# Modulation steps of three parts moved from VectorE to GpSimd, in a two-block transformer kernel

## The reference

```python
c_act = jax.nn.silu(c)
for i in range(DEPTH):                      # 2 layers
    mod = c_act @ ada_w[i] + ada_b[i]       # (1, 1024) @ (1024, 6144)
    shift_t, scale_t, gate_t, shift_c, scale_c, gate_c = split(mod, 6)
    h = rmsnorm(x, norm_g[i, 0]) * (1.0 + scale_t) + shift_t
    y = gla_mixer(h, ...) if i == 0 else diff_mixer(h, ...)
    x = x + gate_t * y
    h = rmsnorm(x, norm_g[i, 1]) * (1.0 + scale_c) + shift_c
    x = x + gate_c * (square(relu(h @ mlp_w1[i])) @ mlp_w2[i])
```

## Time and profile before

| | |
|---|---|
| median of 3 runs | 1410.97 us |
| the profiled execution's own time | 1412.19 us |
| its span, first to last instruction | 1410.4 us |
| mean granted TensorE clock | 0.989 |
| PE, DVE, ACT, POOL busy | 96%, 68%, 47%, 6% |
| chain that ended last | PE 83%, DVE 8%, ACT 3% |

### The profile page before, as it was taken

How to read it: one execution, slowest core, us unless ns; L and a number is a source line. 1 busy time by engine, 2 the same in 40 slices (tenths; PEclk the granted TensorE clock), 3 DMA queues, 4 the chain that set the end, 5 groups by cost and what they waited for, 6 DMA issues and landing times.

```text
span 1410.4 us, 20016 instructions
## 1 busy us (share of the span) xinstructions
PE 1353.2 (96%) x8376; PEld 1188.1 (84%) x8376; DVE 960.2 (68%) x1205; ACT 666.9 (47%) x875; POOL 78.7 (6%) x148
## 2 busy tenths in 40 slices
PE   6899999999999899999899999999999999999997
PEld 1797789998787789998798878999998986999996
DVE  4697787776697876655784445686777545686774
ACT  1553364444456564444534453654545446654542
POOL 1111011110010200000000010000000000000000
PEclk9999999999999999999999999999999999999999
DMA  9787278887393447555265435355553541455530
GB/s 375 272 343 268 90 260 309 297 294 267 122 360 136 161 162 260 209 184 192 102 239 182 176 120 181 148 209 181 190 194 123 214 145 59 151 209 181 188 139 30
DMA packets 46105, 279.41 MB, mean 198 GB/s; under 512 B 5200, under 2 KB 5200, under 8 KB 18880
## 3 DMA queue, kind: packets, MB, share of 16 engines
q1 hardware_dynamic: 33264, 231.57, 44.6%
q0 software_dynamic: 12752, 46.57, 8.8%
HBM read 277.07 MB, written 1.05 MB: 197 GB/s over the span
## 4 chain that ended last, share of the span: by engine, by line
PE 83%; DVE 8%; ACT 3%; issue 2%; DMA 2%; POOL 0%; SPq 0%; POOLq 0%; ACTq 0%; DVEq 0%
PE ps L1658 32%; PE ps L1784 11%; PE ps L1786 11%; PE ps L1785 11%; PE ps L1720 4%; PE ps L1690 3%; DMA ada<-in_ada_w 2%; DVE w_lo L1007 1%; PE ps L2018 1%; DVE acc L1019 1%; PE ps L1846 1%; PE ps L1819 1%; PE ps L1751 1%; ACT w_hi L607 1%; DVE h_lo L1075 1%
## 5 line engine op out<-in xcount | busy, mean ns | idle before, releaser
L1007 DVE TENSOR_TENSOR w_lo<-raw,w_hi 128x2048 fp32r<-128x2048 f32 x210 | 479.4, 2288 | 176.1 <-ACT w_hi L607 175.4
L607 ACT ACTIVATE w_hi<-raw 128x2048 fp32r<-128x2048 f32 x210 | 400.4, 1911 | 203.1 <-PE ps L1658 154.9
L1784 PE MATMUL ps<-h_hi,w_hi 128*128 128x256 f32 x1344 | 381.8, 284 | 1.9 <-ACT m_r L785 1.9
L1786 PE MATMUL ps<-h_hi,w_lo 128*128 128x256 f32 x1344 | 380.3, 283 | 0.0
L1785 PE MATMUL ps<-h_lo,w_hi 128*128 128x256 f32 x1344 | 380.3, 283 | 0.0
L1784 PEld LDWEIGHTS ps<-h_hi,w_hi 128*128 128x128 f32 x1344 | 256.3, 191 | 4.1 <-ACT m_r L785 2.3
L1785 PEld LDWEIGHTS ps<-h_lo,w_hi 128*128 128x128 f32 x1344 | 256.3, 191 | 1.9 <-issue 0.2
L1786 PEld LDWEIGHTS ps<-h_hi,w_lo 128*128 128x128 f32 x1344 | 256.3, 191 | 0.0
L1557 DVE SCALAR_TENSOR_TENSOR f_cv<-ps,cols,f_cv 128x254 f32<-128x254 f32 (+1 forms) x176 | 76.7, 477 | 71.2 <-ACT f_cv L920 69.7
L1658 PE MATMUL ps<-w_hi,hid_hi 128*128 128x512 f32 x368 | 114.5, 392 | 0.0
L1658 PE MATMUL ps<-w_hi,hid_lo 128*128 128x512 f32 x368 | 114.3, 392 | 0.0
(11 more groups left out here) (293 smaller groups left out, 1695.6 us busy)
## 6 DMA issues: line engine op xcount, KB each, us to landing
raw<-in_stream SPq DMA_DIRECT2D x210, 1024.0 KB, 4.8
ada<-in_ada_w POOLq DMA_DIRECT2D x80, 512.0 KB, 5.9
ada<-in_ada_w SPq DMA_DIRECT2D x8, 512.0 KB, 12.6
raw<-in_ada_w SPq DMA_DIRECT2D x8, 512.0 KB, 15.8
row<-in_gate_b POOLq DMA_DIRECT2D x3, 512.0 KB, 3.8
x<-in_x SPq DMA_DIRECT2D x1, 1024.0 KB, 9.7
retc<-in_retc POOLq DMA_DIRECT2D x1, 1024.0 KB, 5.0
out<-xn SPq DMA_DIRECT2D x2, 512.0 KB, 2.7
```

The costliest lines, as they stand in the source:

```text
L607: act.activation(w_hi[:, s, :], raw[:, s, :], ACT.Copy).then_inc(hi_done[s], 1)
L1007: dve.tensor_tensor(w_lo[:, s, :], raw[:, s, :], w_hi[:, s, :].bitcast(f32), ALU.subtract)\
L1784: pe.matmul(out, wh, h_hi[:, kt, :], start=kt == 0, stop=False)
L1786: last = pe.matmul(out, wl, h_hi[:, kt, :], start=False, stop=kt == KT - 1)
```

## The change

The 24 steps of parts 2 to 4 are made by GpSimd, right behind its memset: a product in place in the load's buffer, a wait for it, and an addition to `acc`; the first step of a part is the product alone, into `acc`. After each step GpSimd issues the load that takes the same buffer four steps later. The places where VectorE made these steps are gone. Its remaining steps are one instruction of 128x1024 each, and `ada_half` is gone. TensorE sums part 2 after the first query chunk and part 3 after the second r chunk, ahead of the scores; VectorE finishes part 2 after both query chunks.

```diff
--- before.py
+++ after.py
@@ -258,7 +258,6 @@
         ada_in = [sem(f"ada_in{i}") for i in range(ADA_RING)]
         early_in = [sem(f"early_in{i}") for i in range(2 * NSLOT)]
         ada_more = [sem(f"ada_more{i}") for i in range(ADA_RING)]
-        ada_half = sem("ada_half")
         ada_step = sem("ada_step")
         ada_pe = sem("ada_pe")
         srow_done = sem("srow_done")
@@ -540,14 +539,29 @@
             pool.wait_ge(shp_in, 16)
             norm(0)
 
+            def add_step(s):
+
+                k, place = s % KT, ada[:, s % ADA_RING, :]
+                pool.wait_ge(ada_more[s % ADA_RING], 16 * ((s - 2 * KT) // ADA_RING + 1))
+                if k == 0:
+                    pool.wait_ge(ada_mm, s // KT)
+                    pool.tensor_scalar(acc[:, :], place, csil[:, 0:1], None, ALU.mult).then_inc(ada_step, 1)
+                else:
+                    pc.inc(pool.tensor_scalar(place, place, csil[:, k:k + 1], None, ALU.mult))
+                    pool.wait_ge(pool_chain, pc.n)
+                    pool.wait_ge(ada_step, s)
+                    pool.tensor_tensor(acc[:, :], acc[:, :], place, ALU.add).then_inc(ada_step, 1)
+
             pool.wait_ge(ada_pe, KT)
             for s in range(2 * KT, 2 * KT + ADA_RING):
                 ada_load(s)
 
             pool.wait_ge(hl_done, 4)
             pool.memset(g_q[:, :, :, :, :], 0.0).then_inc(qzero, 1)
-            for s in range(2 * KT + ADA_RING, 5 * KT):
-                ada_load(s)
+            for s in range(2 * KT, 5 * KT):
+                add_step(s)
+                if s + ADA_RING < 5 * KT:
+                    ada_load(s + ADA_RING)
 
             pool.wait_ge(*y_read(Y_GR, 3))
             gate_bias(0)
@@ -1010,14 +1024,12 @@
             def add_step(s, k, place, landed, fill, inc=1):
 
                 dve.wait_ge(landed, fill)
-                for half, done in ((slice(0, 512), ada_half), (slice(512, D), ada_step)):
-                    rows, ck = place[:, half], csil[:, k:k + 1]
-                    if k == 0:
-                        dve.tensor_scalar(acc[:, half], rows, ck, None, ALU.mult).then_inc(done, inc)
-                    else:
-                        dve.wait_ge(done, s)
-                        dve.scalar_tensor_tensor(acc[:, half], rows, ck, acc[:, half], ALU.mult, ALU.add)\
-                            .then_inc(done, inc)
+                if k == 0:
+                    dve.tensor_scalar(acc[:, :], place, csil[:, 0:1], None, ALU.mult).then_inc(ada_step, inc)
+                else:
+                    dve.wait_ge(ada_step, s)
+                    dve.scalar_tensor_tensor(acc[:, :], place, csil[:, k:k + 1], acc[:, :], ALU.mult, ALU.add)\
+                        .then_inc(ada_step, inc)
 
             def steps(first, n):
                 for s in range(first, first + n):
@@ -1221,7 +1233,6 @@
                               bv[:, :, GCH - 1:GCH].to_broadcast([P, GH_ * 4, GCH]), bv, ALU.subtract)\
                 .then_inc(rel_done, 1)
             lo(5)
-            steps(2 * KT, 4)
             lo(6)
             lo(7)
             dve.wait_ge(eb_done, 1)
@@ -1237,22 +1248,16 @@
                                                         GDK ** -0.5, dec[:, :, c, :], ALU.mult, ALU.mult)
                 last.then_inc(c_dve, 1)
                 lo(C_GQ + n + 4)
-                if n == 0:
-                    steps(2 * KT + 4, 4)
+            finish_part(2, 6)
             for n in range(2):
                 dve.wait_ge(*multiplied(C_GK + n))
                 flat = lambda a: a[:, 2 * n:2 * n + 2, :].rearrange("p h t -> p (h t)")
                 dve.tensor_tensor(flat(g_ki), ps[:, 4 + n, :], flat(g_en), ALU.mult)
                 dve.tensor_tensor(flat(g_ks), ps[:, 4 + n, :], flat(g_es), ALU.mult).then_inc(c_dve, 1)
                 lo(C_GK + n + 4)
-                if n == 0:
-                    finish_part(2, 6)
-                steps(3 * KT + 3 * n, 3)
             lo(C_GR + 4)
-            steps(3 * KT + 6, 2)
             finish_part(3, 6)
             lo(C_GR + 5)
-            steps(4 * KT, 2)
 
             for b in range(2):
                 dve.wait_ge(sc_mm, b + 1)
@@ -1272,7 +1277,6 @@
                 dve.scalar_tensor_tensor(st[:, 2, :], st[:, 1, :], el[:, 4 * h + 2:4 * h + 3], kv[2],
                                          ALU.mult, ALU.add).then_inc(st_done, 1)
 
-            steps(4 * KT + 2, 2)
             state(0)
             state(1)
             for b in range(4):
@@ -1297,7 +1301,6 @@
                 last.then_inc(o_done, 1)
             split_stage(TR_GO, h_lo, h_hi)
             lo(C_GR + 7)
-            steps(4 * KT + 4, 4)
             lo(C_GO + 4)
             norm_scale(1, SC_C)
             lo(C_GO + 5)
@@ -1878,14 +1881,15 @@
                 h_rows(C_GV + i, i, 4)
             for n in range(2):
                 cols_chunk(C_GQ + n, 4 + n)
+                if n == 0:
+                    pe.wait_ge(z_done, 1)
+                    sum_part(2, 6)
             for n in range(2):
                 pe.wait_ge(c_dve, n + 1)
                 cols_chunk(C_GK + n, 4 + n)
-                if n == 0:
-                    pe.wait_ge(z_done, 1)
-                    sum_part(2, 6)
             h_rows(C_GR, 0, 4, lambda b: y_read(Y_GV, b))
             h_rows(C_GR + 1, 1, 4)
+            sum_part(3, 6)
 
             pe.wait_ge(c_dve, 4)
             for b in range(2):
@@ -1896,7 +1900,6 @@
                             last = pe.matmul(ps[:, 4 + b, o:o + GCH], g_ki[:, h, t * P:(t + 1) * P],
                                              g_q[:, h, t, c, c * GCH:(c + 1) * GCH], start=True, stop=True)
                 last.then_inc(sc_mm, 1)
-            sum_part(3, 6)
             pe.wait_ge(mod_done, 4)
             for b in range(2):
                 for h in (2 * b, 2 * b + 1):
```

## The result

The changed kernel takes **1481.26 us** (median of 4 runs, 1480.15 to 1483.19) against 1411.28 us for the kernel before beside it: the ratio is 1.0498, 95% interval 1.048 to 1.0516, so 70 us slower. The forecast was 1449, with 1467 as the upper end. The direction and the place were right, the size was not.

The account below looks back on a forecast made before the run. TensorE, busy 96%, was taken as the bound, full VectorE costing it little. Profiled 1412.2 us plus 36.1 for late roots and 2 for the clock gave 1450.3; the profiled run stood 1.2 above the median, so 1449, range 1413 to 1467.

Parts of the forecast that it names:

- the price of GpSimd's product: 128x1024 product in each GpSimd step: 0.91 us from the memset's rate plus 0.19, so 1.1 us.
- TensorE's two answers: Between parts GpSimd waits for TensorE to have read acc: 2.1 us at full clock, 3.5 in a dip.
- 2 us for the clock: Pause before the inverse roots lets the granted clock fall again, costing 0 to 3.4 us; 2 taken.
- The additions: 128x1024 addition into acc in GpSimd's steps: 2.25 us taken, between 1.23 and 2.9.
- The hand-overs: Within GpSimd's steps: 0.1 us for each hand-over, plus 0.53 us for a load's issue.
- The collision: GpSimd reads and VectorE's two-SBUF-input instructions exclude each other, costing GpSimd 31.3 us over parts 2 to 4.
- The place: Loss ahead of the MLP: inverse roots 36.1 us late behind GpSimd's steps, TensorE stalled; later stages keep their length.
- the three stalls: TensorE waits 16.3 us for part 2's sum, 11.1 for part 3's, and a last 8.8 us.
- The prize: About 4.0 us from perfectly removing TensorE's wait around part 3's sum, VectorE's bias addition and the clock dip.
- faster: Rival: GpSimd's steps come in time for sums and roots, giving the 4.0 us; median 1407, chance 0.07.
- half the lock: Rival: collisions cost GpSimd 16 us in place of 31, roots 19.4 us late; median 1432, chance 0.10.
- no collision: Rival: no collision of weight, GpSimd reaches the roots 2.0 us late; median 1413, chance 0.13.

Follow-up runs that it names:

- e13: Kernel before plus eight useless 128x1024 additions on GpSimd from 48 us, ScalarE waiting for the eighth before filling g_v; ratio 1.005 (1.0037 to 1.0062).
- e7: Changed kernel with GpSimd's product written as TENSOR_TENSOR, the column of csil repeated over the row; 1466.28 us in a single run.
- e6: Changed kernel with GpSimd's additions alone, the csil product left out in 21 of 24 steps; 1424.93 us in a single run.
- e9: Kernel before with three of part 2's first four steps moved into VectorE's gap at 58 us; 1410.0 against 1410.13 us, ratio 0.9996.
- e11: Kernel before with GpSimd making only the first four of the 24 steps, the other twenty on VectorE in whole rows; ratio 1.0042 (1.0028 to 1.0056).

## Why the prediction was wrong

**The step that failed** is the price of GpSimd's product: 1.1 us taken, with 1.81 as the high end, and 2.85 measured. I had bounded an instruction that reads and multiplies by a memset, which only writes; the bound from above was none. Over 24 products that is 42 us, more than the miss of 32; the collisions, forecast too high by 16 us, hide a part of it, and that is luck. By the steps of the forecast, up to the roots:

| | forecast | measured |
|---|---|---|
| 24 products, free | 26.4 | 68.4 (24 x 2.85) |
| 21 additions, free | 47.3 | 49.1 (21 x 2.34) |
| hand-overs and 20 issues | 15.7 | 20.5 (rest) |
| TensorE's two answers | 7.0 | 5.8 |
| collisions | 31.3 | 15.4 |
| from 47.2 to the end of part 4 | 127.7 | 159.2 |

Behind the roots I had added 2 us for the clock; the spans leave 0.8 us for it.

**The additions** were right: 2.25 against 2.34 us. The Trainium skill (GPSIMD Engine Reference, 3.1 Elementwise — side-by-side cycle accounting) gives 4497 ns for an addition of 2048 elements; half of it, as an estimate for 1024, is 2.25, and the traces agree within 4%. The same page (4.1 Engine selection) calls an operation with one input roughly line-rate; here the one-input product takes 2.85 us where a memset of the same row takes 0.94 (e13) and the product of e7 with two inputs 1.90, so for this instruction the measurement says otherwise.

**The hand-overs** were taken too short by some 0.25 us a step: 0.30 us pass between the addition's end and the load's issue, where I had 0.1, and the issue is 0.60 us, not 0.53.

**The collision** was the right mechanism, seen from one row of before, and of half the size forecast. I let every two-input instruction of VectorE fall in full on GpSimd. Often GpSimd was first instead: in the changed kernel line 1223, an operation of 0.69 us, takes 2.88, and the scan 4.60 instead of 2.44. In all, VectorE's instructions in the stretch take 13.9 us longer than the same ones before (the 15 w_lo 41.1 instead of 34.0). With GpSimd's 15.4 us that is 29.3: the 31.3 of the forecast were near what the two lose together, and I had put all of it on GpSimd and nothing on VectorE. In the changed kernel VectorE's part is hidden behind TensorE's long waits; in e6 it decides, and the time is 1425 us where GpSimd's chain alone said 1411 to 1418. A w_lo that starts at 76.70, while the product of 74.57 still shows 0.7 us, takes its plain 2.28, so the lock didn't last for the whole span that the profile gives that product. The addition behind it is held to the w_lo's end, 3.69 instead of 2.34:

```profile
70.16 4.60 DVE L1228 TENSOR_TENSOR_SCAN g_b<-shp,g_t 128x256 f32<-128x256 f32 x4
74.79 1.99 DVE L1232 TENSOR_TENSOR g_t<-g_b 128x1024 f32<-128x1024 f32 x1
76.70 2.28 DVE L1021 TENSOR_TENSOR w_lo<-raw,w_hi 128x2048 fp32r<-128x2048 f32 x1
```

**The place** was right: the roots behind GpSimd's steps and the three stalls (forecast 16, 11 and 9 us, measured 23.8, 20.8 and 16.2), the low clock behind them, and the unchanged length of all later stages.

**The prize** of 4.0 us was too high. In e9 the wait is gone and the gain is 0.04%, with an interval that reaches from 0.13% faster to 0.05% slower. I had tied the fall of the clock to that wait; it also comes without it. So the rival "faster" (0.07) had little to win at any speed of GpSimd. No run has a GpSimd that makes all 24 steps in time, but in e11 four steps and in e13 eight useless additions, late for nobody, made the kernel 6 and 7 us slower. The rival "half the lock" had GpSimd's collisions right (16 us), and "no collision" had them too low, but both with my price for the product; neither came near 1481.

## What to carry to other kernels

Price a moved instruction from the same operation on the same engine, and where there is none, say that the upper bound is open: here the product as TENSOR_SCALAR took 2.6 times what I had made of a memset, and a rewrite as TENSOR_TENSOR took a third off. Work on GpSimd that reads SBUF isn't free beside a VectorE that reads two inputs; both lose, and the loss that matters is the one on the way to TensorE. Before moving work off a full engine, test what its relief is worth at all, by placing the work in a gap it already has.

## What the runs showed of the hardware that I had not expected

- TENSOR_SCALAR of 128x1024 float32 on GpSimd takes 2.86 us with a column and 2.78 with a constant (medians); TENSOR_TENSOR with a repeated column takes 1.90, with two full rows 2.34 where nothing is in its way.
- The lock between GpSimd's and VectorE's reads acts both ways. Also VectorE's in-place TENSOR_SCALAR of 128x1024, with one input from SBUF, is held (0.69 to 2.88 us). Three w_lo in a row took 6.67 us with eight GpSimd additions beside them (e13) and 9.17 with GpSimd's steps of e6, so a row of them sometimes keeps GpSimd out and sometimes doesn't.
- The memset, which only writes, and the w_lo beside it kept their durations in the changed kernel (45.40, 1.81 us, and 45.26, 2.28 us).
- The granted clock fell around the sums with no wait ahead of the second one (e9: 0.57 from 116 to 120, the sum at 113.27 right behind the scores).
